# Two activation sums ahead of the FFN norm, a value tile read sooner, and a first down tile whose last k block stands behind three of the second

## The chip, the cores and the metric

The kernel runs on one core of a Trainium2 chip. A core has five engines that run side by side and meet at semaphores: TensorE (PE in the profile, its weight loads PEld), VectorE (DVE), ScalarE (ACT), GpSimd (POOL) and SyncE (SP, which issues the loads of weights). The metric is the device time of one execution in microseconds, the median of several runs; lower is better.

## The reference, cut to what matters

A decoder of two layers runs over 544 tokens (512 of a new sequence and 8 x 4 of running ones). Each layer is a half-step FFN, a mixer of three recurrent branches, and a second half-step FFN; a norm closes the model. The change touches the four FFNs alone:

```python
def rmsnorm(x, g):
    y = xf * lax.rsqrt(jnp.mean(xf * xf, axis=-1, keepdims=True) + EPS)
    return (y * g).astype(x.dtype)

def swiglu_half(x, g, w_up, w_down):
    h = rmsnorm(x, g)
    gate, up = jnp.split(h @ w_up, 2, axis=-1)
    return x + 0.5 * ((jax.nn.silu(gate) * up) @ w_down)

def trunk(x, states, p):
    for l in range(DEPTH):
        x = swiglu_half(x, p['ffn1_norm'][l], p['ffn1_w_up'][l], p['ffn1_w_down'][l])
        y, st = mixer(rmsnorm(x, p['mix_norm'][l]), l, ...)
        x = x + y
        x = swiglu_half(x, p['ffn2_norm'][l], p['ffn2_w_up'][l], p['ffn2_w_down'][l])
    return rmsnorm(x, p['final_norm']), ...
```

The model width is 1024 (8 tiles of 128), the FFN width 2816 (22 tiles of gate and 22 of value).

## The kernel before, in words

**Layout.** Activations stand transposed, 128 features on the partitions and 544 tokens in the free dimension. Every float32 matmul is made of three in the fp32r type: a value is split into a high part (a copy in fp32r) and a low part (value less high part), and a product is high x high + high x low + low x high. So each k block of a tile is six matmuls of 272 tokens (three products, two halves). `Wh`, `Wl` are the parts of a weight tile, `Hh`/`Hl` or `Mh`/`Ml` those of the FFN's input, `Ah`/`Al` those of the hidden tiles.

**Weights.** SP loads weight pieces (up to 512 KB) into two buffers `raw`. POOL's `split` makes `Wh` and `Wl` of a piece in two halves of up to 512 columns (k blocks 0 to 3, then the rest), one copy (L482) and one subtraction (L484) for each, into a ring of two slots. It may start on the piece of tile t+1 when PE has signalled `w_used` in tile t, which PE does once tile t-1 is complete (L539 to L541). PE waits for `w_ready` at k blocks 0 and 4.

**PE's `dense`** computes one tile into one of two PSUM slots (`dps[0]`, `dps[1]`), waits first for that slot (`slot_free`), and tells `tile_done` at the end.

**An FFN** is worked in three blocks of 8, 8 and 6 hidden tiles. In each block PE makes the gate and value tiles, and then eight down tiles (one for each tile of the model width) of 8, 8 or 6 k blocks, whose sums DVE adds into `X`. The first down tile waits before its k block k for hidden tile k (`first`, `ffn_lo`). The down tiles are a loop of two passes of four.

Of the gate and value tiles, most come in steps of two hidden tiles: one pair of dense tiles, and for the other hidden tile a scheme of seven smaller products (`fast`). It needs sums and differences of the input's columns, which an FFN prepares once, in its first block: for k = 0 to 3, ACT's `scaled(k)` puts two tiles of the weighted input into one of two buffers `tx` (by k mod 2), DVE's `combined(k)` makes four sums of 272 tokens out of them, ACT's `combined_hi(k)` and DVE's `combined_lo(k)` make their high and low parts. `scaled(k)` of k = 2, 3 waits for `combined_lo(k-2)`, whose buffer it takes.

**The opening of an FFN** is its first block before that loop: tiles 0 to 3 (gate, value, gate, value). The input is multiplied by the norm's weights only; the norm itself, a number for each token, comes later. PE makes the sums of squares in the middle of tile 1 (`rms`), ACT takes logarithm and exponential (`act_norm`, behind a load of its function table), and DVE multiplies the gate tile by it (`gate_scaled`, which frees PSUM slot 0). Then silu on ACT, `gate` on DVE (times the norm again, for the value), `value` on DVE (which frees slot 1), the high part of the hidden tile on ACT and `hidden_lo` on DVE. All of that stands in a written order on each engine, and the four groups of sums are woven into it.

Of the kernel before, what the change touches and what calls it, by code (L numbers as in the profile page):

```python
# [31 lines left out]
KT = D_MODEL // P  # L32
# [17 lines left out]
FFN_TILES = FFN_PIECES - 2 * FAST  # L50
UP_AT = (2, 18, 34)
DOWN_AT = (10, 26, 40)
FAST_AT = (-1, 3, 7)


# [8 lines left out]
TILES, STREAM = FFN2_T0 + FFN_TILES, FFN2_P0 + FFN_TILES  # L64
# [6 lines left out]
RING = 2  # L71
# [161 lines left out]
def build(nc, wst, xT, par_d, lb_d, const_d, lvm_d, fg_d, st_h, st_g, st_c, st_n, st_m,  # L233
          yT, p_h, p_g, p_c, p_n, s_h, s_g, s_c, s_n, s_m, x_keep):
    ctx = ExitStack()
    with ctx:
# [283 lines left out]

        @block.tensor
        def _(pe):
            def dense(p, t, ring, slot, use, hi, lo, k0, nk, first=None, part=None, opens=None, last=1):


                if part != 1:
                    pe.wait_ge(slot_free[slot], ONE + use)
                for k in range(nk) if part is None else range(part * nk // 2, (part + 1) * nk // 2):
                    if k0 + k in (0, 4):
                        pe.wait_ge(w_ready, p * 2 + (k0 + k) // 4 + 1)  # L530
                    if first is not None:
                        pe.wait_ge(first[0], first[1] + (k + 1))
                    w0 = (k0 + k) * 128
                    for n, (w, x) in enumerate(((Wh, hi), (Wh, lo), (Wl, hi))):
                        for a in range(2):
                            mm = pe.matmul(dps[slot][:, a, 0:HALF], w[:, ring, w0:w0 + 128],  # L536
                                           x[:, k, a * HALF:(a + 1) * HALF],
                                           start=(k == 0 and n == 0), stop=(k == nk - 1 and n == 2))
                    if k == 0 and (k0 == 0 if opens is None else opens):  # L539
                        pe.wait_ge(tile_done, ONE + t)  # L540
                        pe.sem_inc(w_used, 1)  # L541
                if part != 0:
                    mm.then_inc(tile_done, last)

            def rms(n):
# [7 lines left out]
            def ffn(L, t0, p0, norm_no, which):  # L553
# [35 lines left out]
                for b, nf in enumerate((FF_BLOCK, FF_BLOCK, FF_LAST)):  # L589
                    if b == 0:  # L590

                        up(0, 0, (norm_lo, norm_no * KT))
                        up(1, 0, part=0)
                        rms(norm_no)
                        up(1, 0, part=1)
                        up(2, 0)
                        up(3, 0)
                    with pe.Fori(1 if b == 0 else 0, nf // 2) as i:
                        for j in range(2):
                            up(UP_AT[b] + j, i)  # L600
                        fast(L * (2 * FAST) + (which * FAST + FAST_AT[b]) + i)
                    hidden = L * (2 * FF_TILES) + (which * FF_TILES + b * FF_BLOCK)
                    with pe.Fori(0, 2) as i:
                        for j in range(4):
                            t = DOWN_AT[b] + j
                            dense(L * STREAM + (p0 + t) + i * 4, L * TILES + (t0 + t) + i * 4, t % RING, t % 2,
                                  L * (TILES // 2) + (t0 + t) // 2 + i * 2, Ah, Al, 0, nf,
                                  (ffn_lo, hidden) if j == 0 else None)

            def tile(L, t, hi, lo, nk=KT, k0=0, first=None, part=None, opens=None, last=1):  # L610
                g = MIX_T0 + t
# [226 lines left out]
        def _(act):  # L838
# [6 lines left out]
            def act_norm(n):  # L845

                act.preload_act_table_set(LN_EXP)
                act.wait_ge(rms_sum, n + 1)
                ch.sync()
                ch.link(act.activation(halves(tmp[:, 2, :]), SB[:, :, 0:HALF], ACT.Ln, bias=epsc[:, 0:1],  # L850
                                       scale=1.0 / D_MODEL))
                act.activation(tmp[:, 2, :], tmp[:, 2, :], ACT.Exp, scale=-0.5).then_inc(rs_ready, 1)
# [18 lines left out]
            def ffn(L, t0, norm_no, which):  # L871
                weights = par[:, PG["ffn2"]:PG["ffn2"] + KT] if which else wn[:, :]

                def scaled(k):
                    if k > 1:
                        act.wait_ge(t_lo, L * 8 + (which * 4 + k - 1))
                    for a, m in enumerate((k, k + 4)):
                        act.activation(tx[k % 2][:, a, :], X[:, m, :], ACT.Copy,
                                       scale=weights[:, m:m + 1]).then_inc(t_ab, 1)

                def combined_hi(k):
                    act.wait_ge(t_sum, L * 32 + (which * 16 + 4 * k + 4))
                    act.activation(Th[which][:, k, :, :].rearrange("p a b -> p (a b)"),
                                   tx[k % 2][:, 2:4, :].rearrange("p a b -> p (a b)"), ACT.Copy).then_inc(t_hi, 1)

                act.preload_act_table_set(LN_EXP)
                if not which:
                    act.wait_ge(wn_in, L + 1)
                scaled(0)
                act_norm(norm_no)  # L890
                combined_hi(0)
                for b, nf in enumerate((FF_BLOCK, FF_BLOCK, FF_LAST)):
                    if b == 0:
                        for j in range(2):
                            use = L * (TILES // 2) + (t0 // 2 + j + 1)
                            act.wait_ge(slot_free[0], ONE + use)
                            act.activation(tmp[:, 4 + j, :], tmp[:, 4 + j, :], ACT.Silu).then_inc(silu_done, 1)
                            if j == 0:
                                scaled(1)
                            else:  # L900
                                scaled(2)
                                combined_hi(2)
                                scaled(3)
                                combined_hi(3)
                            act.wait_ge(slot_free[1], ONE + use)
                            act.activation(Ah[:, j:j + 1, :], tmp[:, j:j + 1, :], ACT.Copy).then_inc(ffn_hi, 1)
                            if j == 0:
                                combined_hi(1)
                    with act.Fori(1 if b == 0 else 0, nf // 2) as i:
                        n = L * (2 * FAST) + (which * FAST + FAST_AT[b]) + i  # L910
                        for q, src in ((A11, pair[:, 0, :]), (S2, wsum[:, 1, :]), (S1, wsum[:, 0, :]),
# [293 lines left out]
        def _(dve):  # L1205
# [89 lines left out]
            def ffn(L, t0, norm_no, which):  # L1295
# [56 lines left out]
                    dve.wait_ge(prod_done, 7 + n * 7 + k)  # L1352

                combined(0)
                dve.wait_ge(rs_ready, norm_no + 1)
                dve.sem_inc(dve_began, 1)
                for b, nf in enumerate((FF_BLOCK, FF_BLOCK, FF_LAST)):
                    f0 = L * (2 * FF_TILES) + (which * FF_TILES + b * FF_BLOCK)
                    if b == 0:
                        gate_scaled(0, 0)  # L1360
                        combined_lo(0)
                        gate(f0, 0)
                        value(f0, 0, 0)
                        combined(1)
                        hidden_lo(f0, 0, slice(0, 1))
                        gate_scaled(2, 1)
                        combined_lo(1)
                        gate(f0 + 1, 1)
                        combined(2)
                        combined_lo(2)  # L1370
                        combined(3)
                        value(f0 + 1, 2, 1)
                        combined_lo(3)
                        hidden_lo(f0 + 1, 1, slice(1, 2))
                    with dve.Fori(1 if b == 0 else 0, nf // 2) as i:
                        n = L * (2 * FAST) + (which * FAST + FAST_AT[b]) + i
# [552 lines left out]
```

## Time and profile before

| what | value |
|---|---|
| time, median of 3 runs | 3022.28 us (3021.8 to 3024.39) |
| profiled execution | 3033.17 us, its span 3031.4 us |
| mean granted clock of TensorE | 0.989 |
| PE busy | 2964.1 us (98%), 23664 matmuls |
| DVE / ACT / POOL busy | 1602.5 (53%) / 786.5 (26%) / 1752.3 us (58%) |
| chain that ended last | PE 88%, DVE 6%, issue 2%, ACT 2%, POOL 1% |

The profile is one execution seen by the hardware profiler. A busy PE isn't PE at its peak: matmuls overlap, and at the lower of the two clock levels they are busy for longer. "Idle before" is the time in which an engine stood still ahead of an instruction, and the arrow behind it names who ended that wait. The chain of waits is followed back from the last instruction, at each step to what released it.

### The profile page before, as it was taken

The page shows a single profiled execution, that of the slowest core. Times are in us where ns is not written, and L with a number is a line of the kernel's source. Part 1 is how long each engine was busy: PE and PEld are TensorE (multiplying, and loading weights), DVE is VectorE, ACT ScalarE, POOL GpSimd, SP SyncE. Part 2 cuts the span into 40 slices and gives each one's busy share as a digit, 9 for nine tenths or more (in the row PEclk, how much of TensorE's full clock was granted, in tenths as well). Part 3 has the DMA queues.
Part 4 walks back from the last instruction along what each step waited for, and adds up shares of the span by engine and source line. Part 5 has one row for each costly group of instructions (what it writes and reads, how often), then busy time and mean ns, then how long its engine had stood idle before and what let it go on. Part 6 is the DMA issues. An engine that isn't in the chain of part 4 may idle for free.

```text
span 3031.4 us, 65367 instructions
## 1 busy us (share of the span) xinstructions
PE 2964.1 (98%) x23664; PEld 2876.5 (95%) x23664; DVE 1602.5 (53%) x2155; ACT 786.5 (26%) x1296; POOL 1752.3 (58%) x1604
## 2 busy tenths in 40 slices
PE   7999999999999999999999999999999999999998
PEld 7999999989988999999999999999898889999998
DVE  7563665535323467364674736745353245673646
ACT  4221232031232324131241312321303323331212
POOL 5666575545543575656666665654545445766665
PEclk9999999999999999999999999999999999999999
DMA  3232232232221332222232221322312123322231
GB/s 135 79 111 87 70 127 77 67 106 68 82 70 60 106 118 100 88 86 101 74 105 84 90 98 65 125 71 66 114 63 86 63 75 112 108 89 101 80 108 68
DMA packets 115174, 271.22 MB, mean 89 GB/s; under 512 B 9240, under 2 KB 53152, under 8 KB 114720
## 3 DMA queue, kind: packets, MB, share of 16 engines
q1 hardware_dynamic: 65088, 231.76, 22.7%
q10 hardware_dynamic: 49888, 36.71, 4.0%
q8 instruction: 138, 2.26, 0.3%
q14 instruction: 60, 0.49, 0.1%
HBM read 249.92 MB, written 18.52 MB: 89 GB/s over the span
## 4 chain that ended last, share of the span: by engine, by line
PE 88%; DVE 6%; issue 2%; ACT 2%; POOL 1%; ACTq 0%; DMA 0%; PEld 0%; DVEq 0%; POOLq 0%
PE dense L536 64%; PE SA L584 8%; PE SB L584 6%; PE SA L712 1%; PE SA L797 1%; PE SA L698 1%; PE SA L641 1%; PE SA L781 1%; PE SB L793 1%; DVE tmp L1241 1%; DVE Hl L1246 1%; POOL Wl L484 0%; PE SA L683 0%; PE SA L784 0%; PE SA L630 0%
## 5 line engine op out<-in xcount | busy, mean ns | idle before, releaser
L482 POOL TENSOR_SCALAR Wh<-raw 128x512 fp32r<-128x512 f32 x740 | 542.5, 733 | 1037.2 <-PEq L541 935.5
L484 POOL TENSOR_TENSOR Wl<-raw,Wh 128x512 fp32r<-128x512 f32 x740 | 1021.2, 1380 | 61.7
L536 PE MATMUL dense<-Hh,Wh 128*128 128x272 f32 x3104 | 663.0, 295 | 23.6 <-DVE Hl L1232 10.1
L536 PE MATMUL dense<-Hh,Wl 128*128 128x272 f32 x3104 | 648.4, 291 | 0.0
L536 PE MATMUL dense<-Hl,Wh 128*128 128x272 f32 x3104 | 647.9, 290 | 0.0
L536 PEld LDWEIGHTS dense<-Hh,Wh 128*128 128x128 f32 x3104 | 493.7, 191 | 34.8 <-issue 17.6
L536 PEld LDWEIGHTS dense<-Hl,Wh 128*128 128x128 f32 x3104 | 494.9, 191 | 0.0
L536 PEld LDWEIGHTS dense<-Hh,Wl 128*128 128x128 f32 x3104 | 492.9, 192 | 0.0
L536 PE MATMUL dense<-Ah,Wh 128*128 128x272 f32 x1408 | 290.9, 288 | 4.7 <-DVE Al L1333 4.7
L536 PE MATMUL dense<-Ah,Wl 128*128 128x272 f32 x1408 | 289.5, 288 | 0.0
L536 PE MATMUL dense<-Al,Wh 128*128 128x272 f32 x1408 | 289.2, 287 | 0.0
L536 PEld LDWEIGHTS dense<-Ah,Wh 128*128 128x128 f32 x1408 | 219.2, 188 | 5.5 <-DVE Al L1333 5.5
L536 PEld LDWEIGHTS dense<-Al,Wh 128*128 128x128 f32 x1408 | 220.1, 188 | 0.0
L536 PEld LDWEIGHTS dense<-Ah,Wl 128*128 128x128 f32 x1408 | 219.3, 188 | 0.0
L507 POOL TENSOR_TENSOR Sl<-pair,Sh 128x512 fp32r<-128x512 f32 x80 | 123.1, 1539 | 162.7 <-ACT Sh L919 162.7
L1414 DVE SCALAR_TENSOR_TENSOR X<-dense,X 128x544 f32 x64 | 46.4, 725 | 298.5 <-PE dense L536 297.4
L536 PE MATMUL dense<-Mh,Wh 128*128 128x272 f32 x896 | 187.0, 290 | 7.2 <-DVE tmp L1328 5.2
L536 PE MATMUL dense<-Mh,Wl 128*128 128x272 f32 x896 | 185.7, 290 | 0.0
L536 PE MATMUL dense<-Ml,Wh 128*128 128x272 f32 x896 | 185.3, 289 | 0.0
L919 ACT ACTIVATE Sh<-pair 128x512 fp32r<-128x512 f32 x160 | 95.1, 617 | 347.7 <-DMA pair<-wst 347.7
L536 PEld LDWEIGHTS dense<-Mh,Wh 128*128 128x128 f32 x896 | 140.9, 189 | 8.3 <-issue 8.0
L536 PEld LDWEIGHTS dense<-Ml,Wh 128*128 128x128 f32 x896 | 141.1, 189 | 0.0
(423 smaller groups left out, 5246.9 us busy)
## 6 DMA issues: line engine op xcount, KB each, us to landing
raw<-wst SPq DMA_DIRECT2D x336, 512.0 KB, 3.3
pair<-wst SPq DMA_DIRECT2D x80, 512.0 KB, 4.0
raw<-wst SPq DMA_DIRECT2D x32, 384.0 KB, 2.9
x_keep<-X ACTq DMA_DIRECT2D x2, 2176.0 KB, 8.3
X<-x_keep ACTq DMA_DIRECT2D x16, 272.0 KB, 3.1
sst<-st_h ACTq DMA_DIRECT2D x8, 512.0 KB, 4.5
s_h<-sst ACTq DMA_DIRECT2D x8, 512.0 KB, 3.4
sst<-st_c ACTq DMA_DIRECT2D x8, 512.0 KB, 4.0
```

The costliest lines, as they stand in the source:

```text
L482: pool.tensor_scalar(Wh[:, j, cs], raw[:, j, cs], 1.0, 0.0, ALU.mult, ALU.add).then_inc(glink, 1)
L484: pool.tensor_tensor(Wl[:, j, cs], raw[:, j, cs], f32(Wh[:, j, cs]), ALU.subtract).then_inc(glink, 1)
L507: pool.tensor_tensor(Sl[:, q, :], src, f32(Sh[:, q, :]), ALU.subtract).then_inc(q_lo_pool, 1)
L536: mm = pe.matmul(dps[slot][:, a, 0:HALF], w[:, ring, w0:w0 + 128], x[:, k, a * HALF:(a + 1) * HALF], start=(k == 0 and n == 0), stop=(k == ...
L584: mm = pe.matmul(out, w[:, q, k * 128:(k + 1) * 128], xs[:, k, :], start=(opens and k == 0 and m == 0), stop=(k == 3 and m == 2), skip_gro ...
L641: return pe.transpose(out, in_, idn)
L698: mm = pe.matmul(o[s0:e, :, o0:o0 + n * hf].rearrange("p h (n b) -> p h n b", b=hf), K[:, kt(br, hh), c * CH + s0:c * CH + e], qs[:, :, s0 ...
L712: mm = pe.matmul(SA[:, hh // 2, col:col + 64], K[:, kt(br, hh), c * CH:(c + 1) * CH], q, start=True, stop=True)
L781: pe.matmul(SA[:, 0, cs], V[:, h, cs], att[:, h, cs], start=True, stop=(c == 0))
L793: pe.matmul(SB[:, i, :], kts[i * SMP:(i + 1) * SMP, h, :], vblk[i * SMP:(i + 1) * SMP, :], start=True, stop=True)
L919: act.activation(Sh[:, q, :], src, ACT.Copy).then_inc(q_hi, 1)
L1414: STT(xs, dps[j % 2][:, :, 0:HALF], 0.5, xs, ALU.mult, ALU.add).then_inc(slot_free[j % 2], 1)
```

## The change

On PE, `dense` gets a list of k blocks (`ks`) and the k block at which `w_used` is signalled (`signals`, 0 as before). The eight down tiles of a block are written out instead of looped. Tile 0 leaves out its last k block, tile 1 does its first three, tile 0 its last, and tile 1 the rest; tile 1 signals `w_used` at its k block 3, behind the end of tile 0. Tiles 2 to 7 are as before.

On ACT, the opening does `scaled` and `combined_hi` of k = 0 and 1 ahead of `act_norm`, and those of 2 and 3 between the first silu and the second. On DVE, `combined` and `combined_lo` of 0 and 1 stand ahead of the wait for the norm; `combined(2)` and `(3)` come behind the first value tile, and only the two `combined_lo` stand between the third tile's `gate_scaled` and the second `value`.

```diff
+AHEAD = 3
...
-            def dense(p, t, ring, slot, use, hi, lo, k0, nk, first=None, part=None, opens=None, last=1):
+            def dense(p, t, ring, slot, use, hi, lo, k0, nk, first=None, part=None, opens=None, last=1, ks=None,
+                      signals=0):
-                if part != 1:
+                if part != 1 and (ks is None or ks[0] == 0):
                     pe.wait_ge(slot_free[slot], ONE + use)
-                for k in range(nk) if part is None else range(part * nk // 2, (part + 1) * nk // 2):
+                for k in ks or (range(nk) if part is None else range(part * nk // 2, (part + 1) * nk // 2)):
...
-                    if k == 0 and (k0 == 0 if opens is None else opens):
+                    if k == signals and (k0 == 0 if opens is None else opens):
                         pe.wait_ge(tile_done, ONE + t)
                         pe.sem_inc(w_used, 1)
-                if part != 0:
+                if part != 0 and (ks is None or ks[-1] == nk - 1):
                     mm.then_inc(tile_done, last)
...
-                    with pe.Fori(0, 2) as i:
-                        for j in range(4):
-                            t = DOWN_AT[b] + j
-                            dense(L * STREAM + (p0 + t) + i * 4, L * TILES + (t0 + t) + i * 4, t % RING, t % 2,
-                                  L * (TILES // 2) + (t0 + t) // 2 + i * 2, Ah, Al, 0, nf,
-                                  (ffn_lo, hidden) if j == 0 else None)
+                    def down(j, i=0, ks=None, signals=0):
+                        t = DOWN_AT[b] + j
+                        dense(L * STREAM + (p0 + t) + i * 4, L * TILES + (t0 + t) + i * 4, t % RING, t % 2,
+                              L * (TILES // 2) + (t0 + t) // 2 + i * 2, Ah, Al, 0, nf,
+                              (ffn_lo, hidden) if j == 0 else None, ks=ks, signals=signals)
+
+                    down(0, ks=range(nf - 1))
+                    down(1, ks=range(AHEAD), signals=AHEAD)
+                    down(0, ks=range(nf - 1, nf))
+                    down(1, ks=range(AHEAD, nf), signals=AHEAD)
+                    for j in range(2, KT):
+                        down(j % 4, j // 4)
...
                 scaled(0)
+                scaled(1)
+                combined_hi(0)
+                combined_hi(1)
                 act_norm(norm_no)
-                combined_hi(0)
...
                             if j == 0:
-                                scaled(1)
-                            else:
                                 scaled(2)
+                                scaled(3)
                                 combined_hi(2)
-                                scaled(3)
-                                combined_hi(3)
                             act.wait_ge(slot_free[1], ONE + use)
                             act.activation(Ah[:, j:j + 1, :], tmp[:, j:j + 1, :], ACT.Copy).then_inc(ffn_hi, 1)
                             if j == 0:
-                                combined_hi(1)
+                                combined_hi(3)
...
                 combined(0)
+                combined(1)
+                combined_lo(0)
+                combined_lo(1)
                 dve.wait_ge(rs_ready, norm_no + 1)
...
                         gate_scaled(0, 0)
-                        combined_lo(0)
                         gate(f0, 0)
                         value(f0, 0, 0)
-                        combined(1)
+                        combined(2)
                         hidden_lo(f0, 0, slice(0, 1))
+                        combined(3)
                         gate_scaled(2, 1)
-                        combined_lo(1)
+                        combined_lo(2)
                         gate(f0 + 1, 1)
-                        combined(2)
-                        combined_lo(2)
-                        combined(3)
+                        combined_lo(3)
                         value(f0 + 1, 2, 1)
-                        combined_lo(3)
                         hidden_lo(f0 + 1, 1, slice(1, 2))
```

## Rows read from the trace of the kernel before

**Rows 1.** Waits of PE over the span: line, who ended them, us in total, times, longest.

```profile
PE dense L536 <- DVE tmp L1328: 9.1, 4, 2.6
PE dense L536 <- DVE Al L1333: 4.7, 4, 1.2
...
PE dense L536 <- DVE tmp L1319: 3.3, 1, 3.3
...
PE dense L536 <- POOLq L486: 2.1, 1, 2.1
```

**Rows 2.** Chain by pieces: start, us, what; x is the number of matmuls.

```profile
30.43 9.06 PE dense L536 x48
...
114.83 59.84 PE dense L536 x480
...
1162.55 7.79 PE dense L536 x48
```

**Rows 3.** Windows: us, busy of each engine (instructions), granted clock, DMA share, GB/s.

```profile
1163.00:1166.42 3.42, 3.42 (x18) 3.42 (x17) 3.38 (x5) 1.09 (x3) 0.00 (x0) 0.50 0.02 5
1517.99:1521.40 3.41, 2.99 (x24) 2.99 (x24) 1.78 (x3) 1.82 (x3) 2.45 (x2) 1.00 0.50 166
```

**Rows 4.** Timeline, ffn2 of layer 0, all engines: start, duration, engine, line, idle before.

```profile
1132.72 1.28 ACT L847 ACT_TABLE_LOAD   x1
...
1132.77 1.56 POOL L484 TENSOR_TENSOR Wl<-raw,Wh 128x512 fp32r<-128x512 f32 x1
...
1133.21 1.41 DVE L1306 TENSOR_TENSOR tx<-tx 128x272 f32<-128x272 f32 x1
...
1134.90 0.43 DVE L1309 TENSOR_TENSOR tx<-tx 128x272 f32<-128x272 f32 x1
...
1136.15 1.28 POOL L484 TENSOR_TENSOR Wl<-raw,Wh 128x512 fp32r<-128x512 f32 x1
...
1138.34 1.28 POOL L484 TENSOR_TENSOR Wl<-raw,Wh 128x512 fp32r<-128x512 f32 x1
...
1139.10 0.72 ACT L850 ACTIVATE tmp<-SB,epsc 128x544 f32<-128x544 f32 x1 [5.09 <-PE SB L549]
...
1140.41 1.09 ACT L883 ACTIVATE ThH<-tx 128x1088 fp32r<-128x1088 f32 x1
...
1140.74 0.72 DVE L1319 TENSOR_TENSOR tmp<-dense,tmp 128x544 f32<-128x544 f32 x1 [5.41 <-ACT tmp L852]
...
1141.89 0.41 PE L536 MATMUL dense<-Mh,Wh 128*128 128x272 f32 x2
```

**Rows 5.** Timeline, ffn1 of layer 1, all engines.

```profile
1525.17 0.85 DVE L1309 TENSOR_TENSOR tx<-tx 128x272 f32<-128x272 f32 x1
...
1528.73 0.71 ACT L850 ACTIVATE tmp<-SB,epsc 128x544 f32<-128x544 f32 x1 [4.78 <-PE SB L549]
...
1531.47 0.41 PE L536 MATMUL dense<-Hh,Wh 128*128 128x272 f32 x2
```

**Rows 6.** Timeline, ffn1 of layer 0.

```profile
27.84 0.43 DVE L1309 TENSOR_TENSOR tx<-tx 128x272 f32<-128x272 f32 x1
...
28.68 0.66 ACT L852 ACTIVATE tmp<-tmp 128x544 f32<-128x544 f32 x1
```

**Rows 7.** Timeline of PE at tile 5, layer 0's ffn2 and layer 1's ffn1.

```profile
1162.55 0.52 PE L536 MATMUL dense<-Mh,Wh 128*128 128x272 f32 x2 [2.58 <-DVE tmp L1328]
...
1552.17 0.82 PE L536 MATMUL dense<-Hh,Wh 128*128 128x272 f32 x2 [2.50 <-DVE tmp L1328]
```

**Rows 8.** Timeline of PE and POOL, last down block of layer 0's ffn1.

```profile
373.28 0.52 PE L536 MATMUL dense<-Ah,Wh 128*128 128x272 f32 x2 [1.18 <-DVE Al L1333]
...
375.30 1.29 POOL L484 TENSOR_TENSOR Wl<-raw,Wh 128x512 fp32r<-128x512 f32 x1
...
403.11 1.64 POOL L484 TENSOR_TENSOR Wl<-raw,Wh 128x512 fp32r<-128x512 f32 x1
...
405.52 0.41 PE L536 MATMUL dense<-Mh,Wh 128*128 128x272 f32 x2
```


## The prediction

> **What bounds the kernel now.** The page first: TensorE (PE) is busy for nearly the whole span and carries most of the chain that ended last, so only idle time of PE and stretches at a low clock can be won. Next, the waits of PE [rows 1]. The change touches three of them: PE waits 9.1 us, once in each of the four FFNs, for the DVE line L1328 that empties a value tile; 4.7 us, four times, for the last low part of the hidden tiles (Al, L1333); and 3.3 us once for L1319, the first gate tile. Then the chain by pieces [rows 2], for what a tile costs: 480 matmuls take 59.84 us, so a tile of 48 takes 5.98, one k block (six matmuls) 0.75. The same 48 take 9.06 and 7.79 us behind the stops at 30.43 and 1162.55. The windows say why [rows 3]: the granted clock there is 0.50, the lower of the two levels (1.2 GHz), though PE is busy throughout. Behind the stop of 2.1 us that PE took before 1518.41 (it waits there for L486, at the turn of the layer loop) it stays at 1.00. So a stop of 2.6 us costs 1.65 us more (7.79 less 5.98 and the 0.16 us by which the last matmul's end hangs over), one of 2.1 us nothing, and the first FFN's stop of 3.3 us costs 2.9 more.
>
> I call the six tiles of an opening 0 to 5 (gate, value, gate, value, then the first pair of the loop). Even ones use PSUM slot 0, odd ones slot 1, so tile 2 waits for tile 0's gate_scaled (which needs the norm), tile 4 for gate_scaled of tile 2, tile 5 for the value step of tile 3. That last one is the 9.1 us.
>
> **The openings of ffn2 (two, alike).** Before, ScalarE loads the norm's table at 1132.72 and then waits until PE's row sums come; Ln starts at 1139.10, gate_scaled at 1140.74 and ends at 1141.46; PE begins tile 2 at 1141.89 without a stop [rows 4]. The slack is 0.4 us.
>
> After, four things stand ahead of the norm: on ScalarE scaled(1) (it runs beside combined(0)) and two combined_hi (1.09 each), on DVE combined(1) and two combined_lo. Step by step: combined(0) ends as before, at 1135.33; combined_hi(0) runs to 1136.5 beside the next sums. combined(1) is four subtractions of 0.43 us, a little overlapped: some 1.5 us where nothing disturbs them. But the row at 1133.21 took 1.41 us: it ended 0.29 us after the GpSimd operation that began at 1132.77 had (1134.33). While combined(1) will run, GpSimd splits tile 2's weights: two pairs of operations, of which the long ones stand at 1136.15 and 1138.34, the short ones just ahead of them [rows 4]. If DVE and GpSimd take turns, as those two rows do, combined(1)'s first sum goes ahead of the split, the next waits for an operation of 0.62 us, the third for one of 1.28, the fourth for 0.62 again: combined(1) ends near 1138.8 instead of 1136.8 (long ones 1.28 from the rows, short ones 0.6 from the space between them). Then combined_hi(1) to 1139.9, the table load of 1.28, no longer hidden, to 1141.2, Ln 0.75, Exp 0.66 to 1142.7, 0.23 to DVE, gate_scaled 0.72 to 1143.6, and PE: 1.7 us of stop. Without turns combined(1) ends at 1136.8, the table load at 1139.3, and there is no stop. Ends 0 and 1.7 (2.5 were the sums each to take 1.41); I take 1.7, the row's behaviour.
>
> Then the gain. Before, the value step of tile 3 lets PE go only at 1162.55, after 2.58 us [rows 7], because combined(2), combined_lo(2) and combined(3) precede it on DVE. After, silu(0) comes at 1144.0, value(0) ends near 1146.2, combined(2) follows, contended, to 1149.5, combined_hi(2) and the copy of hidden tile 0 (1.09 and 0.66) to 1151.3, hidden_lo and combined(3), contended again by tile 4's split, to 1155.6, gate_scaled(2) to 1156.3. Tiles 2 and 3 run from 1143.6 to 1155.6, so tile 4 now stops for 0.7 us (ends 0 and 1.5, one turn less or more). combined_lo(2), gate(1) and combined_lo(3) follow, and the value step ends at 1161.5, before tile 5 begins at 1162.3: the 2.58 us stop and its 1.65 us at low clock go, with 0.7 us to spare. Sum: 1.7 + 0.7 - 2.58 - 1.65 = **-1.8 us, twice**.
>
> **The opening of layer 1's ffn1.** DVE comes late out of the layer loop: combined(0) ends only at 1526.02, against Ln at 1528.73 and tile 2 at 1531.47 [rows 5]. After: combined(1), among GpSimd's splits, ends near 1530.1, combined_hi(1) 1531.2, table 1532.5, Ln and Exp 1533.9, gate_scaled 1534.9: a stop of 3.5 us (1.0 without turns), followed by low clock (1.65 at least). The slow tiles give tile 4's data time, so that stop is 0.1. Gone: 2.5 and the same 1.65 [rows 7]. Sum 3.5 + 1.65 + 0.1 - 2.5 - 1.65 = **+1.1 us**.
>
> **The first opening.** Here the norm is already late: combined(0) ends at 28.27, Exp begins at 28.68 [rows 6], GpSimd rests. After: combined_hi(0) 28.3 to 29.4, beside it combined(1) to 29.9, combined_hi(1) to 31.0, table 32.3, Ln and Exp 33.7, gate_scaled 34.7, PE 34.85 instead of 30.43: +4.4. Of the low clock's 2.9 us, 2.4 remain, since part of it falls into the stop: -0.5. This FFN's share of L1328, 9.1 - 2 x 2.58 - 2.5 = 1.4, goes. Sum **+2.5 us**.
>
> The four openings: 2.5 - 1.8 + 1.1 - 1.8 = 0.0 us. The work that moves out of the pair's way delays no queue: SP's pair loads and GpSimd's splits follow PE, and the pair's sums come earlier than before.
>
> **The down blocks.** Twelve openings, but only the four of six k blocks stop, 1.18 us each [rows 1, 8]; in the eight of eight k blocks the cover lasts. After, tile 0's five ready blocks, three of tile 1 and tile 0's last run without a stop: tile 0 began 5 x 0.75 and 1.18 us (and a slow start of 0.15) before 373.28, at 368.2; nine blocks end at 374.95, tile 1 at 377.2, where tile 2 began at 378.64: 1.4 us won if its weights are there. They are not. The signal that lets GpSimd split tile 2 waits for tile 0's end, now 0.8 us later (375.1 against 374.3). The first half of that split ended at 376.60; after, it ends at 377.4, and PE starts at 377.6: 1.0 won. And GpSimd has no room to catch up: its first half for tile 2 ended at 376.60, that for the first mixer tile, six tiles later, at 404.75, 28.15 us or 4.69 a tile, where PE needs 4.48. At the block's end it is the bound: the first mixer tile starts at 405.52, and its first half was split by 404.75 [rows 8]; 0.8 us later that is 405.55. So of 1.0 us won early, 0.4 is left at tile 7 and -0.2 at the mixer. Ends -1.4 and +0.3 per block; I take -0.4 for the two ffn2, which nothing follows so closely, and +0.2 for the two ffn1: **-0.4 us in all**. In the eight-k blocks the signal comes 2.25 us later than before, with GpSimd's first half 1.2 us ahead of need by the same durations: nothing. The loops written out save a turn per block; the 59.84 us hold such a turn and no gap [rows 2]: nothing. The Trainium skill ("Runtime: NRT & Kernel Launch", section "Instruction fetch mechanics") says otherwise: a taken branch breaks the prefetch and full unrolling pays where it can be had. By it there would be a gain at each turn; rows 2 show none, and what they could hide is rival 3.
>
> **Sum.** 0.0 - 0.4, say -0.5 us (rounding): the profiled execution's 3033.17 (span 3031.4, 1.8 around it) would be 3032.7. It stands 10.9 us (0.36%) above the median of 3022.28; I carry the difference over unchanged: **3021.8 us, no change**. Under 0.2%, 6.0 us, a measurement can't tell from none.
>
> **Rivals.**
> 1. *Faster: no turns, and weights in time.* ffn2 loses both stops (-4.2 each), layer 1's ffn1 stops for 1.0 at full clock (+1.0 + 0.7 - 4.15 = -2.4), the first stays +2.5, the downs win 1.4 less 0.4 for the wait on weights, four times (-4): -12 us, 3010. For it: many sums of 0.44 us beside a resting GpSimd. Against: 1133.21 and the split's density.
> 2. *Slower: the late norm puts the low clock into every opening.* Place: ScalarE's queue, act_norm behind combined_hi(1). It decides once ffn2's stop passes from 1.7 to beyond 2.1 (the longest that kept full clock). Price: ffn2 2.5 instead of 1.7, plus 1.65, less 0.6 of tile 4's stop, twice (+3.7); a second stretch at low clock, as the first FFN's tile had (2.9 us, nearly twice 1.65), in the other two (1.5 each, +3): 6.7 us over my sum, 3028.5. For it: 0.4 us of distance; against: the turns already counted in full.
> 3. *The written-out loops matter.* Place: the turn of the two-pass loop in each of twelve blocks; price 0.2 us, more than which rows 2 (480 x 0.1247) could not hide; from the first turn on. For it: PE does stop at the layer loop's turn; against: no PE wait stands at a short loop's. 2.4 us, 3019.
>
> **Chances.** Forecast 0.60 (own range 3017 to 3027), rival 1 0.17, rival 2 0.18, rival 3 0.03, others 0.02. Range 3014 to 3029. Faster 0.19 (rival 1 and a tail), slower 0.15 (most of rival 2), same 0.66.
>
> **What would show it.** Right: no PE wait on L1328 and none over 0.4 us on Al; new waits on L1319 in all four FFNs, 1.7 us in ffn2, 3.5 and near 8 in ffn1; PE waiting on GpSimd at tile 2 of the six-k blocks; the table load L847 directly behind the second combined_hi. Wrong: ffn2 without an L1319 wait (rival 1), half clock behind it (rival 2), or tile 5 still waiting.

## The result: slower by a quarter of a per cent, outside the forecast

| | median | lowest to highest | runs |
|---|---|---|---|
| kernel before | 3024.45 us | 3020.83 to 3031.0 | 13 |
| changed kernel | 3033.82 us | 3029.6 to 3038.94 | 13 |

The ratio is 1.0026, with a 95% interval from 1.0017 to 1.0034: 5 to 10 us slower. I had forecast 3021.8 us, no change, within 3014 to 3029.

### The profile page after: what moved, and what is told of

Its sections match the earlier page's. It is cut to its first block and busy times, and to the rows that moved or that the text cites. A ratio compares the mean times of both kernels' runs of the same rounds, so it can differ in the third digit from the quotient of the medians.

```text
span 3033.4 us, 65243 instructions
## 1 busy us (share of the span) xinstructions
PE 2963.7 (98%) x23664; PEld 2872.6 (95%) x23664; DVE 1592.6 (53%) x2155; ACT 786.8 (26%) x1296; POOL 1751.3 (58%) x1604
## 5 line engine op out<-in xcount | busy, mean ns | idle before, releaser
L538 PEld LDWEIGHTS dense<-Hh,Wh 128*128 128x128 f32 x3104 | 493.9, 191 | 39.7 <-issue 22.8
```

## The profile after

The profiled execution took 3035.18 us, its span is 3033.4. The page shows nothing of it: PE is as busy as before, 2963.7 us. The waits do. First those of PE over the span (line, who ended them, us in total, times, longest):

```profile
PE dense L538 <- DVE tmp L1326: 16.4, 6, 8.1
...
PE dense L538 <- POOLq L487: 5.6, 15, 2.5
```

Two of the three waits of [rows 1] that the change touches are gone, those for the value tile and for the last low part. The third, for `gate_scaled` (L1319 before, L1326 now), has grown from one wait of 3.3 us to six of 16.4 in all. And PE waits 15 times for GpSimd's splits (L487), of which 2.5 us is the turn of the layer loop (2.1 before). Where the waits for `gate_scaled` stand, from PE's timeline (start, duration, idle before in brackets), in the first FFN, ffn2 of layer 0 (two stops) and layer 1's ffn1:

```profile
35.33 0.82 PE L538 MATMUL dense<-Hh,Wh 128*128 128x272 f32 x2 [8.05 <-DVE tmp L1326]
...
1143.03 0.51 PE L538 MATMUL dense<-Mh,Wh 128*128 128x272 f32 x2 [1.60 <-DVE tmp L1326]
...
1155.92 0.51 PE L538 MATMUL dense<-Mh,Wh 128*128 128x272 f32 x2 [0.66 <-DVE tmp L1326]
...
1535.21 0.81 PE L538 MATMUL dense<-Hh,Wh 128*128 128x272 f32 x2 [3.76 <-DVE tmp L1326]
```

The forecast had 8, 1.7, 0.7 and 3.5 us at these four places, so the mechanism was read rightly (that the fourth comes so near is partly luck, as shown below). It stands in the timeline of DVE, ACT and POOL in layer 0's ffn2, against [rows 4]:

```profile
1135.09 0.73 DVE L1313 TENSOR_TENSOR tx<-tx 128x272 f32<-128x272 f32 x1
...
1135.62 1.35 POOL L485 TENSOR_TENSOR Wl<-raw,Wh 128x512 fp32r<-128x512 f32 x1
...
1135.75 1.52 DVE L1314 TENSOR_TENSOR tx<-tx 128x272 f32<-128x272 f32 x1
...
1138.11 1.11 ACT L891 ACTIVATE ThH<-tx 128x1088 fp32r<-128x1088 f32 x1 [2.25 <-DVE tx L1316]
...
1139.24 1.28 ACT L855 ACT_TABLE_LOAD   x1
...
1140.53 0.72 ACT L858 ACTIVATE tmp<-SB,epsc 128x544 f32<-128x544 f32 x1
...
1142.17 0.72 DVE L1326 TENSOR_TENSOR tmp<-dense,tmp 128x544 f32<-128x544 f32 x1 [0.60 <-ACT tmp L860]
```

A sum of combined(1) takes 1.52 us beside GpSimd's split instead of 0.43 alone, and ends 0.30 us after GpSimd's operation does; combined_hi(1) waits for the sums, and the table load and Ln stand behind that with nothing to wait for. The Trainium skill ("SBUF — State Buffer", section "Who interferes with whom") says that a DVE instruction with two SBUF inputs contends with a GpSimd instruction that reads SBUF, and that this contention is an exclusive lock; these rows agree, and [rows 4] did.

So the places were right and the total wrong. To see where, I measured each opening (from its first matmul, the first opening from the span's start, to the first one of the fast products) and each down block of six k blocks (from its first matmul to the next stage's first) by the start times of the same matmuls in every trace. The low clock is taken out: 0.45 of PE's busy time in each stretch at 1.2 GHz, where two matmuls start every 0.45 us instead of every 0.25 (where tile 2 stops, only of what lies behind tile 2's start; ahead of it the stop swallows it). "Sum" adds what the four FFNs differ from the profiled execution of before, with the pair steps between; "ratio" is the timed one.

| kernel | openings 1 to 4, us | six-k down blocks 1 to 4, us | sum, us | ratio, interval |
|---|---|---|---|---|
| before | 56.2, 39.7, 39.9, 39.7 | 37.3, 39.6, 37.3, 39.8 | | |
| changed | 59.5, 39.7, 42.4, 39.7 | 38.2, 40.2, 38.2, 40.1 | +8.6 | 1.0026 (1.0017 to 1.0034) |
| e1 openings only | 59.7, 39.7, 38.2, 39.7 | 37.3, 39.7, 37.3, 39.8 | +1.9 | 1.0011 (1.0002 to 1.0020) |
| e2 downs only | 56.4, 39.7, 39.8, 39.7 | 38.2, 40.4, 38.2, 40.1 | +3.2 | 1.0006 (0.9997 to 1.0015) |
| e3 written out only | 56.3, 39.7, 39.9, 39.7 | 37.2, 41.0, 37.1, 39.7 | +1.0 | 1.0011 (1.0002 to 1.0020) |
| e4 before again | 56.2, 39.7, 39.9, 39.7 | 37.3, 39.7, 37.3, 39.7 | 0.0 | 0.9991 (0.9982 to 1.0000) |
| e5 two blocks ahead | 59.4, 39.7, 42.2, 39.7 | 37.5, 39.6, 37.5, 39.3 | +5.6 | 1.0016 (1.0006 to 1.0026) |
| e6 norm table once | 58.3, 39.0, 40.8, 39.0 | 38.2, 40.4, 38.2, 40.1 | +4.6 | 1.0007 (0.9998 to 1.0016) |
| e7 norm first | 56.9, 39.1, 39.3, 39.1 | 37.3, 39.7, 37.3, 39.8 | -1.0 | 0.9994 (0.9985 to 1.0003) |
| e8 norm first, two ahead | 56.9, 39.1, 39.3, 39.1 | 37.5, 39.3, 37.5, 39.4 | -1.5 | 0.9985 (0.9976 to 0.9994) |
| e9 value sooner | 55.5, 39.1, 39.3, 39.2 | 37.3, 39.9, 37.3, 39.8 | -0.9 | 0.9994 (0.9985 to 1.0003) |
| e10 GpSimd relieved | 59.4, 39.7, 42.2, 39.7 | 36.3, 38.2, 36.3, 38.8 | +1.1 | 1.0007 (0.9998 to 1.0016) |
| e11 one block ahead | 59.6, 39.7, 42.2, 39.7 | 37.3, 39.4, 37.3, 39.3 | +5.1 | 1.0008 (0.9999 to 1.0017) |
| e12 value sooner, table once | 56.7, 39.1, 39.2, 39.1 | 37.3, 39.8, 37.3, 39.8 | -0.8 | 0.9997 (0.9988 to 1.0006) |

That the stop swallows a low clock ahead of it shows in layer 1's ffn1. In e10 tile 0 ran at full clock there, and tile 2 stopped for 4.82 us; in the changed kernel tile 0 ran in part at 1.2 GHz, and tile 2 stopped for 3.76. Counted from the opening's start tile 2 began at 18.0 us in e10 and at 18.3 in the changed kernel. The stop in e10, and the windows of tile 0 in the changed kernel and in e10 (the last column but two is the granted clock):

```profile
1534.47 0.68 PE L538 MATMUL dense<-Hh,Wh 128*128 128x272 f32 x2 [4.82 <-DVE tmp L1326]
```

```profile
1516.94:1524.34 7.40, 7.40 (x48) 7.40 (x49) 3.50 (x7) 3.95 (x5) 4.17 (x4) 0.81 0.38 115
```

```profile
1516.43:1522.55 6.12, 6.12 (x48) 6.12 (x49) 2.62 (x4) 3.34 (x5) 4.16 (x4) 1.00 0.30 98
```

The changed kernel's 8.6 us lie within its measured 5 to 10: 3.2 in the first opening, 2.5 in layer 1's ffn1, 2.8 in the down blocks, nothing won in either ffn2. The other sums lie in their intervals too, but for e8, 0.3 us outside. The intervals are 5 to 6 us wide, though, so the timings agree with the sums but can't tell the parts apart; which part costs what rests on the traces, one execution of each kernel. (What lies between an opening and its six-k block, the fast pairs and the blocks of eight k blocks, takes 309.2 us in each ffn1 and 308.7 in each ffn2, in both kernels.)

## The experiments

Each ratio sets a kernel against the kernel before on the same chip.

**e1 and e2: each part alone.** e1 takes the hunks of ACT and DVE, e2 those of PE.

```diff
  e1:   scaled(0)                      e2:  for j in range(KT):  ->
+       scaled(1)                      +    down(0, ks=range(nf - 1))
        combined_hi(0)                 +    down(1, ks=range(AHEAD), signals=AHEAD)
+       combined_hi(1)                 +    down(0, ks=range(nf - 1, nf))
        act_norm(norm_no)              +    down(1, ks=range(AHEAD, nf), signals=AHEAD)
        ...                                 ...
```

> The openings' part alone; the down blocks loop as before. Main theory (both parts lose: the late norm in the two ffn1, and GpSimd pacing in the 6-k down blocks): +2 to +4 us over before, with new PE waits on gate_scaled of about 8, 1.6, 3.8 and 1.6 us, none on the value tile, and no PE wait on GpSimd in the down blocks; the four waits on Al of 1.18 us are back. Rival (the low clock that the trace of before shows behind the old stops is rarer in other executions, so that less is won at tile 5): +5 to +8 us, nearly all of the change's 8 to 9. Rival (written-out loops cost): about 0 to +1.

> The down part alone, openings as before. Main theory: tile 2 of the 6-k blocks starts about 1.4 us earlier, then PE waits on GpSimd 0.2 to 0.9 us at several tiles, and each of the four blocks ends 0.3 to 1.0 us later than before: +2 to +4 us. Rival (the openings carry nearly all): 0 to +1.5. Rival (written-out loops cost fetch time): +4 or more.

Both parts cost time in their traces: e1 +1.9 us and e2 +3.2 (e2's timed interval includes no change). Together they cost 3.5 more than apart. The difference is layer 1's ffn1: 38.2 us in e1, where tile 2 does not stop, and 42.4 in the changed kernel. Not all of it is the change: in e1 tile 0 ran at low clock, which brought PE to tile 2 1.5 us later. At full clock the table load, which ended 0.87 us before Ln began, would have set the norm instead of the row sums, and tile 2 would have stopped for some 0.7 us (an estimate from e1's timeline), which makes the opening 38.9. DVE's combined(0), last sum, and combined(1) there, in the changed kernel, with the split that began in between:

```profile
1524.97 0.85 DVE L1316 TENSOR_TENSOR tx<-tx 128x272 f32<-128x272 f32 x1
...
1525.62 1.36 POOL L485 TENSOR_TENSOR Wl<-raw,Wh 128x512 fp32r<-128x512 f32 x1
...
1525.74 1.54 DVE L1311 TENSOR_TENSOR tx<-tx 128x272 f32<-128x272 f32 x1
1527.32 0.77 DVE L1313 TENSOR_TENSOR tx<-tx 128x272 f32<-128x272 f32 x1
1528.00 1.52 DVE L1314 TENSOR_TENSOR tx<-tx 128x272 f32<-128x272 f32 x1
1529.44 0.43 DVE L1316 TENSOR_TENSOR tx<-tx 128x272 f32<-128x272 f32 x1
```

and in e1, where GpSimd's next split begins at 1523.66, as the last sum does:

```profile
1522.48 0.43 DVE L1303 TENSOR_TENSOR tx<-tx 128x272 f32<-128x272 f32 x1
1522.95 0.44 DVE L1305 TENSOR_TENSOR tx<-tx 128x272 f32<-128x272 f32 x1
1523.31 0.43 DVE L1306 TENSOR_TENSOR tx<-tx 128x272 f32<-128x272 f32 x1
1523.66 0.43 DVE L1308 TENSOR_TENSOR tx<-tx 128x272 f32<-128x272 f32 x1
```

In every kernel with the new down blocks DVE leaves the layer loop later against PE (combined(0) begins 6.6 to 6.9 us behind PE's restart, in all others 5.0 to 5.6): the last steps of the down block run beside a split that has moved (the copy `wn`, 0.47 us in e1, takes 1.13). That delay puts combined(1) among the splits.

**e3 and e4: the loops written out in the old order, and the kernel before again.**

```diff
- with pe.Fori(0, 2) as i:
-     for j in range(4):
+ for j in range(KT):
+     down(j % 4, j // 4)
```

> The eight down tiles written out, in their old order, nothing else. Main theory and first rival: within 1 us of before, same PE waits on Al. Rival (written-out loops cost): +3 us or more. The opposite rival (turns of the loop cost): -2.4 us.

> The kernel before once more, for a second trace and for span and granted clock of each execution. Main theory: ratio 1.000, half clock behind the tile-5 stops in most openings again (at least two of three), the differences between executions explained by the number of stretches at low clock. Rival (low clock in the openings is rarer): a trace with at most one of the three.

In e3 the three blocks ahead of no layer turn are 0.1 to 0.2 us shorter; the one ahead of it is 1.4 longer, since the turn grows. Here PE's first matmul behind it:

```profile
1518.15 0.52 PE L538 MATMUL dense<-Hh,Wh 128*128 128x272 f32 x2 [3.63 <-DVE Hl L1236]
```

It is 2.1 to 2.4 in the kernels that keep the loop, 2.4 to 2.6 in the interleaved ones, except 1.7 where GpSimd is relieved. Why it grows with the tiles written out in the old order, the traces don't show. The Trainium skill's rule that full unrolling pays ("Runtime: NRT & Kernel Launch", section "Instruction fetch mechanics") is not borne out beyond those 0.1 to 0.2 us: the sum is +1.0 us, the timing agrees in sign. e4 shows three things. Timed against itself the kernel before reads 0.9991, so a ratio that far from 1 is no gain yet. Two executions of it differ by 5.4 us of span (3031.4 and 3026.0), and 5.1 of it is the clock by the measure above, in the mixers too. And with the same stops, of the last three openings, which with their low clock took 41.3, 41.4 and 41.3 us in the profile of before, only one does so in e4 (41.1); the others take 39.9 and 39.7.

**e5, e10, e11: what paces the six-k blocks.** From the changed kernel, one line each in e5 and e11:

```diff
- AHEAD = 3
+ AHEAD = 2          (e5; 1 in e11)
```

and in e10, whose products of the last two k blocks use stale weights:

```diff
...
- run(p0 + DOWN_AT[b], p0 + DOWN_AT[b] + KT, nf * P)
+ run(p0 + DOWN_AT[b], p0 + DOWN_AT[b] + KT, nf * P, (0,) if b == 2 else (0, 1))
```

> The changed kernel with two k blocks of the second down tile ahead of the first one's last instead of three (AHEAD 2). Theory GpSimd: in the six-k blocks TensorE now follows GpSimd's splits, which the third block delays by 0.75 us, and the halves that TensorE waits for run beside DVE. Two blocks (1.5 us) still cover the old stop of 1.18 us; the signal comes 0.75 us sooner. Expected: the 15 waits on GpSimd (5.6 us in all, of which 2.5 is the layer's turn) shrink to under 1.5 us beside the turn, each six-k stage goes from 38.2 to 37.5 us or less (37.3 before), in all 2 to 3 us won on the changed kernel, ratio to the kernel before 1.0015 to 1.002. Rival, that DVE beside GpSimd alone sets the pace, wherever the signal stands: stages stay at 38.2, ratio 1.0026. Rival, that two blocks are too few: a wait on the last low part (Al) of 0.1 to 0.4 us comes back.

> The changed kernel with one k block ahead (AHEAD 1). Theory: the stage's length follows the signal that gives GpSimd the weight slot. Counted in k blocks of 0.75 us from the block's start it comes at 7 blocks and 1.18 us before (6.4 us), at 10 blocks with three ahead (7.5), at 9 with two (6.75), and with one ahead again at 7 blocks and 1.18 us, since the stop of 0.43 us that is left keeps tile 0's end where it was. Expected: a wait on the last low part of 0.4 us, and the six-k stages at 37.2 to 37.4 us like before, though the stop is 0.75 us shorter. Rival, that what TensorE's stop loses is what counts: 36.6. Ratio with the late norm left in: 1.001 to 1.0015.

> The changed kernel where GpSimd doesn't split the second half (the last two of six k blocks) of the six-k down blocks' weights: some 1.2 to 1.8 us of its 4.7 us a tile left out, so the products of those k blocks use stale weights. Theory GpSimd: in these blocks GpSimd, not TensorE, sets the pace, which is why filling TensorE's stop of 1.18 us won nothing. Expected: no wait on GpSimd in the block, the stage at 35.9 to 36.3 us (38.2 in the changed kernel, 37.3 before), so the stop's 1.18 us is won once GpSimd has room; in all 4 x 2 = 8 us less than the changed kernel, ratio 1.000. Rival, that the interleaved order itself costs TensorE (two accumulations alternating): 38.2 as before.

GpSimd paces them. Its first split behind the signal, in layer 0's ffn1, in the kernel before and with three, two and one k block ahead:

```profile
374.59 0.63 POOL L482 TENSOR_SCALAR Wh<-raw 128x512 fp32r<-128x512 f32 x1 [3.64 <-PEq L541]
```

```profile
377.27 0.62 POOL L483 TENSOR_SCALAR Wh<-raw 128x512 fp32r<-128x512 f32 x1 [4.61 <-PEq L543]
```

```profile
377.62 0.62 POOL L483 TENSOR_SCALAR Wh<-raw 128x512 fp32r<-128x512 f32 x1 [3.84 <-PEq L543]
```

```profile
377.79 0.62 POOL L483 TENSOR_SCALAR Wh<-raw 128x512 fp32r<-128x512 f32 x1 [3.64 <-PEq L543]
```

The block begins at 368.19, 370.06, 371.17 and 371.55 us, so this split begins 6.4 us into it before, and 7.2, 6.5 and 6.2 with three, two and one ahead: 0.8 later, as late, and 0.2 earlier. (The count in the second expectation, 1.07, 0.32 and 0 later, has the order right.) The block takes 38.2, 37.5 and 37.3 us, which is 0.9, 0.1 and 0 longer than before. With one block ahead 0.9 of the 1.18 us stop is filled (the rest in the fence) and the block is as long as before:

```profile
PE dense L538 <- DVE Al L1340: 1.1, 4, 0.3
```

Relieve GpSimd, and the same order gives 36.3: the stop is won, as the edit meant, and one short wait is left. e5's waits on GpSimd fell less than I expected, to 2.5 us beside the turn. What they cost is more than their idle time. A stop of the kernel before, and one of the changed kernel, each with the rows around it (pairs of matmuls start 0.25 us apart where nothing stops):

```profile
371.69 0.41 PE L536 MATMUL dense<-Ah,Wl 128*128 128x272 f32 x2
373.28 0.52 PE L536 MATMUL dense<-Ah,Wh 128*128 128x272 f32 x2 [1.18 <-DVE Al L1333]
373.64 0.41 PE L536 MATMUL dense<-Al,Wh 128*128 128x272 f32 x2
```

```profile
378.80 0.41 PE L538 MATMUL dense<-Ah,Wl 128*128 128x272 f32 x2
379.37 0.52 PE L538 MATMUL dense<-Ah,Wh 128*128 128x272 f32 x2 [0.16 <-POOLq L487]
379.73 0.42 PE L538 MATMUL dense<-Al,Wh 128*128 128x272 f32 x2
```

From the first row to the third pass 1.95 and 0.93 us, where 0.50 would do: 1.45 for an idle time of 1.18, and 0.43 for 0.16. Each stop costs 0.27 us beside its idle time: 0.16 because the last pair, which takes 0.41, has nothing to overlap with, and 0.11 because the next pair starts 0.36 behind the first one instead of 0.25. The five of this block, 1.06 us idle, cost 2.28 (summed over all starts more than 0.16 us apart); the old single one cost 1.46.

And GpSimd's work comes beside DVE's. Here the long operation of a first half, which PE waits for, and that of a second half, in the changed kernel; before, the first took 1.29 in the block's first split [rows 8] and the second 1.09. So the half that PE waits for has become longer, and not GpSimd's work as a whole:

```profile
387.62 1.62 POOL L485 TENSOR_TENSOR Wl<-raw,Wh 128x512 fp32r<-128x512 f32 x1
...
389.93 0.74 POOL L485 TENSOR_TENSOR Wl<-raw,Wh 128x256 fp32r<-128x256 f32 x1
```

**e6: the norm's table load left out** (the load at the FFN's start has put the same table in place).

```diff
...
-                act_norm(norm_no)
+                act_norm(norm_no, load=False)
```

> The changed kernel without the second load of the norm's table (1.28 us on ScalarE, behind the two combined_hi) in the FFN openings; the load at the FFN's start has put the same table in place. Theory late norm: ScalarE's queue ahead of Ln sets when tile 2 may begin, so all four stops at tile 2 lose 1.28 us: 8.05 to 6.8, 1.6 to 0.3, 3.76 to 2.5, 1.6 to 0.3, in all 5.1 us or 0.17% of the time, ratio 1.0005 to 1.0015. Rival, that PE's row sums or DVE set the norm: the stops stay as they are and the ratio at 1.0026.

The stops became 5.0, 0.9 and 1.9 us, with the 0.66 at tile 4 unchanged. ffn2's fell by 0.7 only, because DVE's two `combined_lo` then end last and hold `gate_scaled`. The first fell by more than the load's 1.28, since a low clock in tile 1 brought PE there 1.5 us later. ScalarE's queue is confirmed as what delays the norm; 1.2 us go in the first opening, 1.6 in layer 1's ffn1, 0.7 in each ffn2, and the ratio falls to 1.0007.

**e7 and e8: the norm first.** e7 is e1 with the norm ahead again; e8 adds down blocks with two ahead and a kept loop for the other three pairs of tiles.

```diff
  ACT  scaled(0)                        DVE  combined(0)
       scaled(1)                             combined(1)
-      combined_hi(0)                   -    combined_lo(0)
-      combined_hi(1)                   -    combined_lo(1)
       act_norm(norm_no)                     dve.wait_ge(rs_ready, ...)
+      combined_hi(0)                        gate_scaled(0, 0)
+      combined_hi(1)                   +    combined_lo(0)
                                        +    combined_lo(1)
       ...                                   ...
```

> The kernel before with the new opening order in all but one thing: the norm stands ahead of both combined_hi and both combined_lo again; the down blocks are the old ones. Theory: the new order's gain (tile 5 no longer stops, 2.5 us three times and 1.4 once) is real and was paid away by the late norm. Expected: tile 2's stops as before (none in ffn2, 0 to 0.5 in layer 1's ffn1, 3.3 in the first), none over 0.3 at tile 5, at tile 4 up to 0.7: openings of 37.5 to 38.2 us where they were 39.7 to 41.3, in all 6 to 9 us less, ratio 0.997 to 0.998. Rival, that the opening's work only moves and some later tile waits as long (DVE's sums beside GpSimd are the same work in either order): the openings stay at 39.5 and the ratio at 1.000. Rival low clock: the stop stays away and the low clock with it, 0.996.

> The same openings with the norm first, and the down blocks opened with two blocks ahead as in the first of these runs, the other three pairs of down tiles in a loop of three instead of written out. If written-out code lengthens the layer's turn, the turn is 3.7 to 3.9 us here, as in the kernel before (4.4 in the changed one, 5.5 with the old down order written out). If the openings win 6 to 9 us and the six-k blocks stand within 0.3 us of before, ratio 0.9965 to 0.998; if two blocks ahead win the 0.4 us per block that I had forecast, 0.9965; if the down opening costs 0.9 us per block whatever its signal, 0.999.

e7's gain in each of the last three openings is 0.6 us, not 2: tile 2 and tile 5 don't stop, and tile 4 does, 1.97 us in ffn2, since its `gate_scaled` now stands behind combined(3):

```profile
1151.69 0.52 PE L536 MATMUL dense<-Mh,Wh 128*128 128x272 f32 x2 [1.97 <-DVE tmp L1318]
```

The first opening costs 0.6 more, since scaled(1) still stands ahead of the norm on ScalarE and tile 2 stops for 4.58 us instead of 3.31. The rival was nearer. e8, at 3021.4 us, is the one version that beats both kernels by more than its interval (ratio 0.9985, where e4's was 0.9991); the sum of its stages explains a third of it. Its turn is 2.3 us, as in the other kernels that keep a loop. (The expectation's 3.7 to 3.9 count the turn in another way, as what the six-k block ahead of it takes beyond eight tiles of 4.48 us; so counted it is 3.5.)

**e9 and e12: the value step alone, and with the table load left out.**

```diff
                         combined(2)
+                        value(f0 + 1, 2, 1)
                         combined_lo(2)
                         combined(3)
-                        value(f0 + 1, 2, 1)
```

> The kernel before with one edit: the value step that frees slot 1 for tile 5 stands directly behind combined(2) on DVE, ahead of combined_lo(2) and combined(3), which need not come first. DVE idles 1.2 us at that place before (it waits for ScalarE's combined_hi(2)), so the step costs nothing there. Theory: tile 5's stop (2.5 us in the second to fourth opening, 1.4 in the first) goes and nothing takes its place, since the norm is untouched: openings of 37.2 to 37.5 us where they were 39.7, the first 1.4 less; in all 8 to 9 us less, the low clock behind the old stops besides; ratio 0.9970, and within 0.996 to 0.998. Rival, that the sums put behind it come too late for the first fast products: a wait of PE on DVE or t_lo of 0.5 to 2 us at the products, the opening at 38.5 to 39.7, ratio 0.999 to 1.

> The first of these runs and the norm's second table load (1.28 us) left out of the FFN openings. Theory: in layer 0's ffn1 that load stands between scaled(0) and Ln with PE's row sums long done, so tile 2's stop there falls by 1.28 us less what combined's sums take from it, 0.8 to 1.3 us; in the three others ScalarE waits for the row sums behind the load, and nothing changes. Ratio 0.0003 to 0.0004 below the first run's, 0.9966. Rival, that GpSimd and DVE set the first norm too: no difference between the two runs.

The rival held. Tile 5 no longer stops, and the first fast product does, for the pair's weights (L1349), which DVE makes after all sums. PE's waits in e9, and that stop in layer 0's ffn2:

```profile
PE SA L584 <- DVE Sl L1349: 7.1, 4, 2.1
```

```profile
1167.88 0.39 PE L584 MATMUL SA<-Mh,Sh 128*128 128x272 f32 x1 [2.11 <-DVE Sl L1349]
```

In e12 the first opening's stop at tile 2 falls from 3.31 to 1.91 us, and that at its first product grows from 0.88 to 3.32. (e9's 55.5 for this opening is likely too low: 1.5 us are taken off for a low clock in tile 2 that the stop at the product would in part have swallowed; e12 had none there.) Wherever the order lets a stop go, DVE's remaining work meets PE a few tiles on: 2.58 us in ffn2 before, 1.60 + 0.66 after, 1.97 in e7, 2.11 in e9, 0.92 + 0.66 in e6.

## Why the prediction was wrong, by its own steps

Three terms failed: the low clock that I took off in ffn2, the gain that I put down for the six-k blocks, and the cost of layer 1's ffn1. Most of the stops that I worked out stand in the trace; much of what was to pay for them didn't come.

- **The openings of ffn2, -1.8 us each: failed by its low-clock term.** The stops are those forecast (1.60 and 0.66 against 1.7 and 0.7, no wait at tile 5). But 1.65 of the 1.8 was the low clock behind tile 5's stop, read as a rule from [rows 3]; in the four traces of kernels with the old opening (before, e2, e3, e4) it stood behind 7 of 12 such stops in the last three openings, and an opening without it takes 39.7 us before and after. The 0.15 that was left is eaten by the second stop's 0.27. That is 3.6 us of the miss. Over all four openings the low clock took 5.4 us on the mean of those four traces and 3.9 on that of five with the new order (changed, e1, e5, e10, e11): 1.5 less, where I had taken off 3.8.
- **The first opening, +2.5: right in kind, short in size.** The stop is 8.05 us as worked out; with the clock taken out it costs 3.2 (0.3 of it a later first matmul), where I had 3.0 and then took off 0.5 for it.
- **Layer 1's ffn1, +1.1: too small, and its stop right by luck.** Without the clock it costs 2.5. I had combined(1) ending 11.7 us behind the opening's start; it ended at 12.9, because the down block delays DVE, which I hadn't named. (Without that delay, in e1, the opening wins 1.7, or some 1.0 with tile 0 at full clock.) So the stop would have been some 5.0 us (3.76 and the 1.3 that the low clock in tile 0, behind the layer's turn, delayed PE), and e10, with tile 0 at full clock, has 4.82. My 3.5 met the 3.76 because the two errors cancel.
- **The six-k blocks, -0.4 in all: failed.** They cost +2.8 us. I had GpSimd as the pace and the signal 0.8 us late, both of which the traces show, and then credited 0.4 us for each ffn2; and I counted PE's waits by their idle time, when several short ones each cost 0.27 more, and left out that the first halves would run beside DVE (1.62 instead of 1.29).
- **The eight-k blocks, nothing: right.** **The loops, nothing: nearly**; the interleaved order's turn is 0.2 to 0.5 us longer, in the 2.8 above. Rival 3's gain shows in three of e3's six-k blocks, 0.1 to 0.2 us each, but e3's sum has the other sign.
- **The rivals.** Rival 1 lost to the turns of DVE and GpSimd, which stand in every trace. Rival 2's sign was right and its mechanism wasn't: ffn2's stop stayed at 1.6 us at full clock:

```profile
1143.03:1146.45 3.42, 3.42 (x27) 3.42 (x28) 2.36 (x4) 3.41 (x6) 2.77 (x3) 1.00 0.00 0
...
1535.21:1538.60 3.39, 3.39 (x15) 3.39 (x16) 2.67 (x4) 3.11 (x5) 2.75 (x3) 0.50 0.01 2
```

(windows behind the stops at 1143.03 and 1535.21; the granted clock is 1.00 and 0.50).
- **Carrying the 10.9 us between profile and median over: failed with the first point.** The execution profiled of before was one with much low clock, so what the change removes of that is not removed from the median.

In all: -0.5 forecast, +8.6 found; ffn2 +3.6, first opening +0.8, layer 1's ffn1 +1.4, down blocks +3.2.

e3's ratio is higher than its sum of 1.0 us, and e8 wins three times its sum. In both the clock makes the difference. Each execution on record has a mean granted clock: 0.9898 on the mean of e3's and 0.9908 on that of the kernel before beside it, 0.9922 for e8 and 0.9907 for the kernel before beside that. Among the executions of the kernel before, 0.001 of clock goes with some 2.5 us. So by this estimate 2.6 of e3's mean difference of 3.4 us are clock, which leaves 0.9, and 3.7 of e8's 4.7, which leaves 1.0 won. (The mean counts low clock inside stops too, which costs nothing, so this is rough.) Why e3 has more low clock and e8 less stays open.

## What to carry to other kernels

When work is moved ahead of a stop on an engine that is itself the pace (DVE beside GpSimd here), look for where the stop will stand next, because the work has not become less: e9 removed a 2.5 us stop and got one of 2.1 a tile later. Before pricing a stop on TensorE, ask whether another engine's queue would hold the next tile anyway, and count each stop with its restart. When the low clock is taken out of a stretch, leave in what lies ahead of a stop that another engine ends. And take no clock effect from one execution as part of what a change will win.

## What the runs showed of the hardware that I had not expected

- A stop of TensorE cost 0.27 us more than its idle time shows, whether it lasted 0.16 us or 1.18: 0.16 of lost overlap and 0.11 of a slower start.
- Whether the low clock follows a stop isn't told by its length here. Behind the 2.5 us stops at tile 5 it stood 7 times in 12, behind e9's and e12's stops of 2.0 to 2.1 at the first product of the last three openings 5 times in 6, behind the 1.97 at tile 4 in e7 and e8's ffn2 in none of 4, behind the 1.6 of ffn2 in the changed kernel, e1, e5, e10 and e11 in none of 10. My rule from the turn (2.1 us cost nothing, [rows 3]) fell with it: the low clock stood behind the turns of 2.27 us in e7 and 2.32 in e8, not behind e3's of 3.63.
- With the eight down tiles written out in their old order the layer loop's one turn took 3.63 us against 2.1 to 2.4, though nothing in the turn itself was changed. One trace shows it, and not why; the interleaved order, written out too, has 2.4 to 2.6.
